# Weight sums made in memory ahead of time, and a last feed-forward part computed as seven products

## The reference

```python
u = jax.nn.relu(rmsnorm(x, norm_ffn) @ w_ff1)   # 512 x 1024 @ 1024 x 4096
return x + (u * u) @ w_ff2                      # 512 x 4096 @ 4096 x 1024
```

## Time and profile before

| | us |
|---|---|
| three timed runs | 2909.05, 2911.4, 2911.43 |
| profiled execution, device time | 2907.8 |
| its span | 2905.7 |
| PE busy | 2872.8 (99%) |
| DVE busy | 1673.4 (58%) |
| ACT busy | 1214.1 (42%) |
| POOL busy | 73.1 (3%) |

### The profile page before, as it was taken

How to read it: one execution, slowest core, us unless ns; L and a number is a source line. 1 busy time by engine, 2 the same in 40 slices (tenths; PEclk the granted TensorE clock), 3 DMA queues, 4 the chain that set the end, 5 groups by cost and what they waited for, 6 DMA issues and landing times.

```text
span 2905.7 us, 38576 instructions
## 1 busy us (share of the span) xinstructions
PE 2872.8 (99%) x16126; PEld 2372.1 (82%) x16130; DVE 1673.4 (58%) x2442; ACT 1214.1 (42%) x1863; POOL 73.1 (3%) x62
## 2 busy tenths in 40 slices
PE   7999999999999999999999999999999999999999
PEld 6878887888887777888888877888888877888887
DVE  7776666645255566533334764566674664656673
ACT  5655422235233333522224465454443465444432
POOL 0000011200000000000000000000000000000000
PEclk9999999999999999999999999999999999999999
DMA  8443355633432222233323222224422222234422
GB/s 308 170 129 117 116 189 181 199 124 102 95 94 73 73 74 66 82 93 109 97 91 100 83 73 74 87 102 131 130 88 95 88 73 73 95 109 130 129 74 87
DMA packets 224509, 319.89 MB, mean 110 GB/s; under 512 B 16496, under 2 KB 123344, under 8 KB 223568
## 3 DMA queue, kind: packets, MB, share of 16 engines
q1 hardware_dynamic: 207520, 266.96, 28.8%
q0 software_dynamic: 11744, 48.24, 5.2%
q10 hardware_dynamic: 5072, 2.23, 0.3%
HBM read 308.98 MB, written 2.11 MB: 107 GB/s over the span
## 4 chain that ended last, share of the span: by engine, by line
PE 95%; DVE 3%; ACT 2%; issue 1%; DMA 0%; ACTq 0%; DVEq 0%
PE G L2383 49%; PE G L2390 18%; PE G L2442 5%; PE G L2336 4%; PE G L2425 4%; PE X L2336 3%; PE X L2709 1%; PE X L2487 1%; PE G L2408 1%; PE X L2723 1%; PE X L2809 1%; PE X L2819 1%; PE G L2765 1%; PE X L2720 1%; PE G L2525 0%
## 5 line engine op out<-in xcount | busy, mean ns | idle before, releaser
L2383 PE MATMUL G<-u_hi,w_hi 128*128 128x512 f32 x2096 | 836.5, 399 | 7.5 <-issue 7.5
L2383 PE MATMUL G<-u_hi,w_lo 128*128 128x512 f32 x2096 | 818.7, 391 | 0.0
L2383 PE MATMUL G<-u_lo,w_hi 128*128 128x512 f32 x2096 | 818.2, 390 | 0.0
L1425 DVE TENSOR_TENSOR w_lo<-raw,w_hi 128x2048 fp32r<-128x2048 f32 (+3 forms) x214 | 481.0, 2249 | 458.1 <-ACT w_hi L747 457.1
L747 ACT CAST w_hi<-raw 128x2048 fp32r<-128x2048 f32 (+3 forms) x218 | 409.5, 1879 | 455.3 <-DMA raw<-in_w_ff 175.5
L2383 PEld LDWEIGHTS G<-u_hi,w_hi 128*128 128x128 f32 x2096 | 394.4, 188 | 94.8 <-issue 15.3
L2383 PEld LDWEIGHTS G<-u_hi,w_lo 128*128 128x128 f32 x2096 | 394.2, 188 | 85.1
L2383 PEld LDWEIGHTS G<-u_lo,w_hi 128*128 128x128 f32 x2096 | 394.8, 188 | 79.0 <-issue 1.4
L2223 DVE TENSOR_TENSOR hid_f<-silu_g,G 128x512 f32<-128x512 f32 x44 | 30.1, 688 | 163.4 <-PE G L2383 150.1
L1544 DVE SCALAR_TENSOR_TENSOR acc<-ada_raw,cond,acc 128x512 f32<-128x512 f32 x140 | 105.2, 752 | 12.6 <-DMA ada_raw<-in_ada_w 3.9
L2425 PE MATMUL G<-u_hi,w_hi 128*128 128x256 f32 x384 | 109.3, 285 | 2.8 <-DVE u_lo L1690 2.8
(11 more groups left out here) (512 smaller groups left out, 4763.7 us busy)
## 6 DMA issues: line engine op xcount, KB each, us to landing
raw<-in_ffn_w_in SPq DMA_DIRECT2D x88, 512.0 KB, 4.8
ada_raw<-in_ada_w POOLq DMA_DIRECT2D x40, 1024.0 KB, 5.7
raw<-in_w_ff SPq DMA_DIRECT2D x80, 512.0 KB, 4.3
raw<-in_w_in SPq DMA_DIRECT2D x56, 512.0 KB, 4.2
raw<-in_attn_w_in SPq DMA_DIRECT2D x96, 256.0 KB, 3.7
raw<-in_ffn_w_out SPq DMA_DIRECT2D x40, 512.0 KB, 4.6
raw<-in_hgrn_w_in SPq DMA_DIRECT2D x32, 512.0 KB, 5.4
raw<-in_attn_w_in SPq DMA_DIRECT2D x24, 512.0 KB, 4.7
```

The lines of the kernel that those rows point to most:

```text
L1425: tt(w_lo[slot][:, 0:nk, 0:w], raw[slot][:, 0:nk, 0:w], w_hi[slot][:, 0:nk, 0:w].bitcast(F32), ALU.subtract).then_inc(s_lo, 1)
L2383: ins = mm(G[0:c1_ - c0, m, :], w[iw][:, k, c0:c1_], xs[ix][:, x0(b) + kk, :], start=first, stop=last, skip_group_check=True)
```

## The change

- All seven chunks of a part with seven products are now loaded into `raw` by SP and split like any other chunk. `weights_upper`, `weights_lower` and `quadrant_loads` are gone. Three of the seven chunks are quarters of `w_ff2`; four are sums.
- The four sums of a part are made in memory (`weight_sums`, an internal tensor) by eight transfers that GpSimd issues, of 1 MB each: four copies and four that accumulate. They are issued for the seven parts at the starts of `at_qk0`, `at_qk1`, `at_qk2`, `ffn_in10`, `ffn_in11`, `ffn_out11` and `z0`. SP waits for a part's sums ahead of its sum chunks.
- The last part of the last layer is computed as seven products too: `ff_in13` goes through `hidden_part` and `hidden_sums`, and `ff_st13` takes the place of `ff_out13`. The last part of the first layer stays plain.
- The three additions of `first_product` stand behind product 3 of the layer's last part with products, no longer behind product 6. The result is written in four transfers that follow the additions.

```diff
             add(f"ff_in{l}{q}", 2, KT, "act")
-            if q < FF_PARTS - 1:
+            if (l, q) == (0, FF_PARTS - 1):
+                add(f"ff_out{l}{q}", 2, KT, "dve")
+            else:
                 add(f"ff_st{l}{q}", 1, KT, None)
-        add(f"ff_out{l}{FF_PARTS - 1}", 2, KT, "dve")
...
+                if g["evictor"] is None and s in sum_of:
+                    sp.wait_ge(s_wsum, 128 * (g["group"] + 1))
...
-            last = plan[order[-1]]["mine"]
-            sp.wait_ge(s_free["dve"], last + 4)
-            sp.dma_start(by_token[:, :, 0:512], h[:, :, 0:512]).then_inc(s_out, 16)
-            for j in range(TB):
-                sp.wait_ge(s_free["dve"], last + 4 + j + 1)
-                sp.dma_start(by_token[:, j, 512:1024], h[:, j, 512:1024]).then_inc(s_out, 16)
-            sp.wait_ge(s_out, 16 * (1 + TB))
+            last = 14 * plan[order[-1]]["group"]
+            for added, rows, cols in ((10, slice(2, 4), upper_columns), (12, slice(0, 4), lower_columns), (13, slice(0, 1), upper_columns),
+                                      (14, slice(1, 2), upper_columns)):
+                sp.wait_ge(s_add, last + added)
+                sp.dma_start(by_token[:, rows, cols], h[:, rows, cols]).then_inc(s_out, 16)
+            sp.wait_ge(s_out, 64)
...
-                    pool.wait_ge(s_wsum, 3 * q + 2)
-                    pool.wait_ge(s_lo, c0 + B21 + 1)
-                    pool.dma_start(W21, W11, accum_op=ALU.add).then_inc(s_fourth, 16)
+
+            def sums_of_weights(q):
+
+                of = {(k, n): quadrant(q, k, n) for k in range(2) for n in range(2)}
+                to = {x: sums[q, i] for x, i in sum_of.items()}
+                pool.wait_ge(s_wsum, 128 * q)
+                pool.dma_start(to[B12_22], of[0, 1]).then_inc(s_wsum, 16)
+                pool.dma_start(to[B11_12], of[0, 0]).then_inc(s_wsum, 16)
+                pool.dma_start(to[B_SUM4], of[1, 0]).then_inc(s_wsum, 16)
+                pool.wait_ge(s_wsum, 128 * q + 48)
+                pool.dma_start(to[B12_22], of[1, 1], accum_op=ALU.add, max_dma_last_dim=8192).then_inc(s_wsum, 16)
+                pool.dma_start(to[B11_12], of[0, 1], accum_op=ALU.add, max_dma_last_dim=8192).then_inc(s_wsum, 16)
+                pool.wait_ge(s_wsum, 128 * q + 80)
+                pool.dma_start(to[B_SUM3], to[B11_12]).then_inc(s_wsum, 16)
...
+            for q, name in enumerate(("at_qk0", "at_qk1", "at_qk2", "ffn_in10", "ffn_in11", "ffn_out11", "z0")):
+                pool.wait_ge(s_tile, plan[name]["t0"])
+                sums_of_weights(q)
...
-            def weights_lower(c, q, i):
-
-                if i == B12_22:
-                    for j in range(2):
-                        dve.wait_ge(s_quad[j], 64 * (q + 1))
-                    tt(W12, W12, W22, ALU.add).then_inc(s_wsum, 1)
-                    dve.wait_ge(s_wsum, 3 * q + 1)
-                    dve.wait_ge(s_lo, c)
-                    tt(W11, W11, W12, ALU.add).then_inc(s_wsum, 1)
-                dve.wait_ge(s_hi, c + 1)
-                tt(w_lo[c % SLOTS][:, :, :], weights_of[i], w_hi[c % SLOTS][:, :, :].bitcast(F32), ALU.subtract).then_inc(s_lo, 1)
-                if i == B21:
-                    dve.wait_ge(s_lo, c + 1)
-                    dve.wait_ge(s_wsum, 3 * q + 2)
-                    tt(W12, W11, W22, ALU.subtract).then_inc(s_wsum, 1)
...
-                if int(name[-1]) == FF_PARTS - 2:
-                    dve.wait_ge(s_add, 14 * q + 14)
+                    if s == 3 and name in (f"ff_st0{FF_PARTS - 2}", f"ff_st1{FF_PARTS - 1}"):
+                        dve.wait_ge(s_add, 14 * q + 8)
```

More of the change, by code:

```diff
@@ L192, in gemm_plan, with build @@
     return plan, order, c
-def build(nc, a, out, gates, where1, where2, where3, stop=None):
+def build(nc, a, out, gates, sums, where1, where2, where3, stop=None):
     plan, order, n_chunks = gemm_plan()
@@ L594, in source, with quadrant @@
                 return one(a["w_ff1_2"][int(name[-2])], off=int(name[-1]) * D)
+            if name.startswith("ff_st"):
+                i, q = k0 // 4, plan[name]["group"]
+                if i in sum_of:
+                    return [(0, sums[q, sum_of[i]].rearrange("(t p) n -> p t n", p=P)[:, k0 % 4:k0 % 4 + k1 - k0, :])]
+                return [(0, quadrant(q, *quadrant_of[i]).rearrange("(t p) n -> p t n", p=P)[:, k0 % 4:k0 % 4 + k1 - k0, :])]
             return one(a["w_ff2_2"][int(name[-2])])
+        def quadrant(q, kh, nh):
+            l, part = part_of(q)
+            return a["w_ff2_2"][l][1024 * part + 512 * kh:1024 * part + 512 * kh + 512, 512 * nh:512 * nh + 512]
         def first_row_tile(name):
@@ L1462, in products_added @@
                         ins.then_inc(s_add, 1)
-                if int(name[-1]) == FF_PARTS - 2:
-                    dve.wait_ge(s_add, 14 * q + 14)
-                    for j, cols, op in ((0, second, ALU.subtract), (2, first, ALU.add), (2, second, ALU.subtract)):
-                        n.give(tt(h[:, j:j + 2, cols], h[:, j:j + 2, cols], first_product[:, :, :], op), s_dve)
-                    n.own(s_dve)
+                    if s == 3 and name in (f"ff_st0{FF_PARTS - 2}", f"ff_st1{FF_PARTS - 1}"):
+                        dve.wait_ge(s_add, 14 * q + 8)
+                        for j, cols, op in ((0, second, ALU.subtract), (2, first, ALU.add), (2, second, ALU.subtract)):
+                            n.give(tt(h[:, j:j + 2, cols], h[:, j:j + 2, cols], first_product[:, :, :], op), s_dve)
+                        n.own(s_dve)
             def hidden_sums(name):
@@ L2267, in _ @@
                     products_added(name)
[L2268 removed]
+                elif name.startswith("ff_in") and name != f"ff_in0{FF_PARTS - 1}":
                     hidden_sums(name)
@@ L3022, in make @@
     gates = nc.dram_tensor("gates", (4, D), F32, kind="Internal").ap()
-    build(nc, aps, out, gates, where1, where2, where3, stop)
+    sums = nc.dram_tensor("weight_sums", (2 * FF_PARTS - 1, 4, 512, 512), F32, kind="Internal").ap()
+    build(nc, aps, out, gates, sums, where1, where2, where3, stop)
     return arrays
```

65 lines of the change are left out of this document (12 added, 53 removed).

## The result

The changed kernel takes 2955.18 us (median; 2948.79 to 2957.57) against 2911.41 us before (2909.05 to 2912.57): 1.0148 times the time, interval 1.0130 to 1.0166. 2933.0 was predicted, with 2917 to 2947 as the range. The direction was right; the time lies 22 us above the forecast and 8 us above the range.

The account below looks back on a forecast made before the run. TensorE, 95% of the chain, was taken as the bound. Terms -5.45 + 17.4 + 8.8 + 1.2 + 1 = +22.9 us on the profiled 2907.8 gave 2930.7; 2.3 added for the timed median made 2933, range 2917 to 2947.

Parts of the forecast that it names:

- The matmuls: Last quarter as seven products, 168 matmuls instead of 192: minus 5.45 us, with the end keeping its shape.
- The stalls: In hidden_part, chunk 1's cast waits for its load ahead of evictions; TensorE waits before product 2, seven groups, plus 17.4 us.
- The walk: Step-by-step times around block 1's end E, from chunk 1's cast to chunk 2's w_lo, ready 2.46 us late.
- The clock: Lower TensorE clock after the stalls: five of seven lose it, 1.75 us each, plus 8.8 us, bounds 0 and 12.3.
- Additions moved: Three additions behind product 3 make product 6 wait for its bank, 0.6 us in two groups: plus 1.2 us, 0 to 2.
- main case: Stalls before product 2 with most of the clock drops: 2927 to 2939 us, chance 0.53.
- The sums in memory: GpSimd's transfers slow loads in attention, eight casts at 0.5 us each, some slack: plus 1 us, bounds 0 and 8.
- The memory sums slow the loads in attention: Rival: each of eight waiting casts in attention waits as much again, 23.6 us, on top; 2940 to 2960 us, chance 0.12.
- The prediction's own sign of being wrong: Wrong if TensorE passes product 2 without a wait, or ScalarE's landing waits in attention grow well past 23.6 us.

Follow-up runs that it names:

- e10_head_too: e9_both with the second chunk's split also behind the third tile in the first block of each feed-forward input; 2900.04 us, 0.9968 of before.
- e2_split_later: Changed kernel with the split of chunk 1 of the seven products, in block 1, behind the evictions of tiles 0 and 1; 2937.07 us, 1.0086 of before.
- e7_all_splits_moved: Changed kernel with chunk 1's split behind tiles 0 to 2, the next ahead of tile 3's upper and lower parts, three additions behind product 4; 2930.39 us, 1.0066.
- e9_both: e7_all_splits_moved plus memory sums in quarters, one in flight; two of the three additions moved to product 3, five writes at the end; 2906.49 us, 0.9984 of before.
- e8_quarter_pieces: Changed kernel with the memory sums in pieces of 256 KB, one in flight at a time, at the same places; 2932.86 us, 1.0080 of before.

## Why the prediction was right and wrong

**The matmuls: right.** Seven products stand in the place of 192 matmuls, and the end is as said: an addition of 0.69 us and one small write, 2.5 us in all. With the order repaired the 5.45 us come out whole (e10_head_too).

**The stalls: right.** Predicted were a wait for w_lo before product 2 in seven groups, 2.48 us each, 17.4 in all; it is 7 times, 16.9 us. The walk holds in its steps: product 2 at 2659.52 less the stall of 2.34 and 10.88 gives E = 2646.3; the cast is at E-6.0 (E-5.83 predicted), the square of tile 2 at E+2.3 (E+2.5), and w_lo of chunk 2 at E+10.9 (E+11.05). Two slips in the working are small: three sums of 0.46 us from E-0.29 end at E+1.09, not E+0.89, and the bounds of landing give 15.6 to 19.1 us, not 19.3.

**The clock: right in size, by luck.** The 1.75 us that the sum counts for each of five stalls are the 23.51 us of the 96 matmuls behind the 2.75 us gap less four times 5.44. The first matmul behind the 1.89 us took 0.47 us, behind the 1.99 and 2.75 us 0.77 and 0.76; over the two microseconds there (474:476, 27:29, 2592:2594) the granted clock was 1.00, 0.51 and 0.54. Product 2 took 7.27, 5.73, 7.32 us in layer 0 and 5.73, 7.19, 5.73, 7.34 in layer 1. Four of seven ran on at half clock (granted 0.50 to 0.52 of full speed over two microseconds, 1.00 behind the other three), not five, at some 1.8 us each, and the other three lost 0.3: 8.2 us where 8.8 were predicted. Nothing in the rows before said which stalls would lose it, so that the sum came out is luck.

**Additions moved: nearly right.** Product 6 is late by 0.52 and 0.58 us in the two groups named, where 0.6 each was predicted, and by 0.32 us in one more. Each such start costs 0.3 us besides (5.70 for 5.44).

Together the two feed-forward stages grew by 12.6 + 10.6 + 5.45 = 28.7 us before the product left out is taken off; 17.4 + 8.8 + 1.2 = 27.4 were predicted. The kernel without sums, at 2937.5, lies in the prediction's main case (2927 to 2939). In the profiled executions the whole is 41.2 us for 22.9: 13.9 us are missing in the sums in memory, 1.3 in the feed-forward stages, and 3.2 lie in the start and the first layers, which vary by as much.

**The sums in memory: the step that failed.** Plus 1 with bounds of 0 and 8 was taken; the stages say 14.9 us, the medians 15.4 to 17.7. The prediction's own length for the eight transfers, some 55 us, was near: 48 to 59 us pass between the first and the last issue of a group, and the last then takes some 8. SP passes its wait at once, as predicted. Wrong was the price for a load beside them. I took 0.5 us from loads that ran beside GpSimd's loads of `ada_w`, and carried it over to transfers of 1 MB from memory to memory, two or three at once. These put three to four times as many packets beside a load (51 and 66 for each engine, against 17), and one load under a pair took 17 us, not 5.5. The upper bound of 8 was as wrong as the value: nothing in the rows taken bounded what one load can wait, while one that lands just in time ahead of a stage's head has no slack.

**The rival had the cause, not the place.** "The memory sums slow the loads in attention" (chance 0.12, 2940 to 2960) gave the right time for half a reason. That the sums slow the loads is so: in the rows of the queues a load's packets of 0.5 KB, 0.03 to 0.04 us each, took turns with GpSimd's of 0.17 us. In attention ScalarE's waits for landing grew from 23.6 to 73.6 us, as it said, but TensorE lost 1.3 us there in the profiled execution. 3.9 us went in feed-forward 1 and 9.7 in mixer 0, the latter with 7.2 us of stall and half clock behind it. Two of the seven groups, outside attention, made most of the loss. The prediction's own sign of being wrong, waits for landing in attention well past 23.6 us, came true; but the idle time of TensorE that it looked for in attention lay in the other stages. With the same transfers attention lost 7.7 us in e2_split_later and 3.5 in e7_all_splits_moved, and feed-forward 1 lost 7.5 and 6.5, so these stages are near an edge that moves from execution to execution. This may be why after's profiled execution (2948.8) is 6 us below its median; that was not tried.

**How a load waits, and what stays open.** Two readings were possible: a load waits until the transfers ahead of it have ended, or the engines share their time unevenly between the queues. In 1606:1609 both queues moved 249 packets, and GpSimd's took 90.3% of the engines' time and the load's 20.9% (the two overlap a little). So it is the second reading there: the queues moved as many packets as each other, and a turn of GpSimd's, 0.17 us, is four times as long as one of the load's, 0.04. It isn't all: the load issued at 1598.12 had its first packets in 1602:1603, some 4 us later, where a load of the kernel before, issued at 1595.56, had them within 1 us. That start is not explained. No run varied the size of a load's packets, so the share of each is read from the trace and not shown by an experiment. Open too is why four of seven nearly equal stalls lost the clock, and why the gap at the head of `ff_in10` is longer in e9_both than before.

## What to carry over

Price a background transfer by the longest time that one foreground load can spend under it, at the stage where a load lands last in time, and not by a mean slowdown: here 17 us, where 0.5 was taken. The profile gives what is needed for that: the packets queued for each engine and the time of one. Keep such transfers small and one at a time: in quarters of 256 KB (e8_quarter_pieces) the three stages were back within 0.1 us each, where after lost 14.9 us in them. When data that lay in SBUF comes by a load, look at what stands behind its cast in the engine's program: the cast belongs behind the work that is already due. The product left out was worth its 5.45 us only with both in order, as in e9_both and e10_head_too; the sums in memory themselves never paid.

## What the runs showed of the hardware

- Two accumulating transfers of 1 MB in memory, in flight together (five of after's seven groups), took 16 to 19 us from the first issue to the end of GpSimd's wait, and the DMA engines, 99% busy in 1597:1614, moved 198 GB/s; in 2744 to 2746 they moved 316 GB/s at 82%. Transfers of 256 KB, one in flight, landed in 4.1 us (median of 168, e8_quarter_pieces).
- Where both queues had work, the DMA engines took SP's and GpSimd's in turn, packet by packet, whatever a packet held in these two stretches: 249 and 249 in 1606:1609, 244 and 247 in 819:822. Packets of 2 KB that accumulate and of 4 KB that copy both took an engine 0.17 us, those of 0.5 KB of a load 0.03 to 0.04 us.
- In after seven stalls of 2.3 to 2.9 us lie in front of the same matmuls. Four lost the clock, three did not, and their length doesn't tell them apart. PE's rows after the four stalls of layer 1, idle time in brackets:

```profile
2659.52 0.50 PE L2299 MATMUL X<-w_hi,hidden_sums_hi 128*128 128x512 f32 x1 [2.34 <-DVE w_lo L1404]
2743.72 0.79 PE L2299 MATMUL X<-w_hi,hidden_sums_hi 128*128 128x512 f32 x1 [2.31 <-DVE w_lo L1404]
2829.48 0.50 PE L2299 MATMUL X<-w_hi,hidden_sums_hi 128*128 128x512 f32 x1 [2.41 <-DVE w_lo L1404]
2913.74 0.53 PE L2299 MATMUL X<-w_hi,hidden_sums_hi 128*128 128x512 f32 x1 [2.34 <-DVE w_lo L1404]
```

Three stretches behind the last three of them; the granted clock is the third number from the end:

```profile
2744.00:2746.00 2.00, 2.00 (x5) 0.50 0.82 316
2830.00:2832.00 2.00, 2.00 (x10) 1.00 0.66 254
2915.00:2917.00 2.00, 2.00 (x6) 0.50 0.26 101
```

  After 2.31 us the granted clock was 0.50 of full speed in 2744:2746 and the first matmul took 0.79 us; after 2.41 us they were 1.00 in 2830:2832 and 0.50 us. After one stall of 2.34 us the clock was 1.00 (2660:2662), after the other 0.52 (2914:2916), with a first matmul of 0.53 us.
